# One number in a hand-made instruction order: the scan's positions scaled by 0.75 against attention's

## What is computed

```python
def step(s, inp):                    # one chunk of tokens
    kc, vc, lf = inp[0], inp[1], inp[2]
    cum = jnp.cumsum(lf, axis=2)
    last = cum[:, :, -1:, :]
    s_new = jnp.exp(last[:, :, 0, :])[..., None] * s + \
        jnp.einsum('bhsd,bhse->bhde', kc * jnp.exp(last - cum), vc)
    qc = inp[3]
    o_inter = jnp.einsum('bhtd,bhde->bhte', qc * jnp.exp(cum), s)
    decay = jnp.exp(jnp.where(mask, cum[:, :, :, None, :] - cum[:, :, None, :, :], -jnp.inf))
    att = jnp.einsum('bhtd,bhsd,bhtsd->bhts', qc, kc, decay)
    return s_new, o_inter + jnp.einsum('bhts,bhse->bhte', att, vc)

# per layer, for direction forward and back
mix = jnp.concatenate([fx, ax, rx], axis=-1) @ w_out[l]   # Fourier, attention, scan
```

## Time and profile before

| | us |
|---|---|
| median of 3 executions | 3174.1 (3170.85 to 3175.51) |
| the profiled execution, its own time | 3190.28 |
| its span, first to last instruction | 3188.5 |
| PE, weight loads, DVE, ACT, POOL busy | 2676.0, 2005.8, 783.6, 809.0, 829.6 |

### The profile page before, as it was taken

One profiled execution on the slowest core, in us unless ns is written; L12 is line 12 of the kernel. 1 busy time (PEld: TensorE's weight loads), 2 busy tenths in 40 slices (PEclk: granted clock), 3 DMA queues, 4 the chain that ended last, 5 costly groups with the idle time before them and its releaser, 6 DMA issues.

```text
span 3188.5 us, 38162 instructions
## 1 busy us (share of the span) xinstructions
PE 2676.0 (84%) x16726; PEld 2005.8 (63%) x16726; DVE 783.6 (25%) x1326; ACT 809.0 (25%) x1018; POOL 829.6 (26%) x310
## 2 busy tenths in 40 slices
PE   1898887999995987788769999999695767699997
PEld 0686555777773873334558888888583433577785
DVE  0102323244223004453330111111202453311111
ACT  1232223122123223222232112111323332322222
POOL 0241231333330210233212222222130133244442
PEclk9898898999997997756789999999897778899999
DMA  6231023334441110000201111111011000222221
GB/s 138 99 133 47 21 84 141 140 152 177 156 143 52 53 45 2 1 1 1 79 27 67 53 67 67 53 60 60 27 53 46 1 1 15 92 80 93 104 88 47
DMA packets 42524, 220.55 MB, mean 69 GB/s; under 512 B 4025, under 2 KB 12873, under 8 KB 18933
## 3 DMA queue, kind: packets, MB, share of 16 engines
q1 hardware_dynamic: 35192, 200.52, 17.3%
q10 hardware_dynamic: 7164, 17.57, 2.3%
HBM read 212.05 MB, written 6.03 MB: 68 GB/s over the span
## 4 chain that ended last, share of the span: by engine, by line
PE 70%; DVE 9%; ACT 5%; issue 2%; DMA 1%; POOL 1%; ACTq 0%; DVEq 0%; POOLq 0%
PE PS L590 52%; PE PS L507 2%; PE PS L593 2%; PE PS L935 2%; PE PS L959 2%; PE PS L922 2%; DVE small L1017 1%; PE PS L941 1%; DVE tmp L533 1%; DVE a_lo L525 1%; DVE a_lo L1572 1%; PE PS L1519 1%; PE PS L625 1%; PE PS L1630 1%; DVE hid_lo L766 1%
## 5 line engine op out<-in xcount | busy, mean ns | idle before, releaser
L1758 POOL TENSOR_TENSOR w_lo<-raw,w_hi 128x2048 fp32r<-128x2048 f32 (+1 forms) x146 | 648.5, 4442 | 1653.9 <-ACT w_hi L661 1653.9
L590 PE MATMUL PS<-a_hi,w_hi 128*128 128x512 f32 (+1 forms) x2104 | 678.9, 367 | 162.5 <-DVEq L342 99.7
L590 PE MATMUL PS<-a_lo,w_hi 128*128 128x512 f32 (+1 forms) x2104 | 677.2, 366 | 0.0
L590 PE MATMUL PS<-a_hi,w_lo 128*128 128x512 f32 (+1 forms) x2104 | 674.6, 365 | 0.0
L590 PEld LDWEIGHTS PS<-a_hi,w_hi 128*128 128x128 f32 x2104 | 359.8, 191 | 243.0 <-issue 170.6
L661 ACT ACTIVATE w_hi<-raw 128x2048 fp32r<-128x2048 f32 (+1 forms) x146 | 270.3, 1851 | 523.9 <-PE PS L590 339.9
L590 PEld LDWEIGHTS PS<-a_hi,w_lo 128*128 128x128 f32 x2104 | 360.7, 191 | 66.7
L590 PEld LDWEIGHTS PS<-a_lo,w_hi 128*128 128x128 f32 x2104 | 359.9, 191 | 62.9
L590 PE MATMUL PS<-hid_hi,w_hi 128*128 128x512 f32 (+1 forms) x784 | 269.3, 380 | 36.2 <-DVE hid_lo L766 32.8
L590 PE MATMUL PS<-hid_lo,w_hi 128*128 128x512 f32 (+1 forms) x784 | 266.7, 377 | 0.0
L590 PE MATMUL PS<-hid_hi,w_lo 128*128 128x512 f32 (+1 forms) x784 | 266.2, 376 | 0.0
(11 more groups left out here) (193 smaller groups left out, 2834.5 us busy)
## 6 DMA issues: line engine op xcount, KB each, us to landing
raw<-in_w_ada SPq DMA_DIRECT2D x48, 1024.0 KB, 7.0
raw<-in_w_ff SPq DMA_DIRECT2D x32, 1024.0 KB, 4.8
raw<-in_w_in SPq DMA_DIRECT2D x27, 1024.0 KB, 4.8
raw<-in_w_gate SPq DMA_DIRECT2D x22, 1024.0 KB, 4.7
raw<-in_w_up SPq DMA_DIRECT2D x22, 1024.0 KB, 4.7
raw<-in_w_down SPq DMA_DIRECT2D x16, 1024.0 KB, 4.7
raw<-in_w_out SPq DMA_DIRECT2D x12, 1024.0 KB, 5.0
raw<-in_w_down SPq DMA_DIRECT2D x8, 768.0 KB, 4.2
```

Of the source, the lines that this page charges most:

```text
L590: mm = p.matmul(ps[:, dst], wv[:, k, idx * P:(idx + 1) * P], av[:, k, dst], start=first, stop=last)
L1758: pool.tensor_tensor(w_lo[:, m % 2, 0:kt, 0:ncol], src, w_hi[:, m % 2, 0:kt, 0:ncol].bitcast(F32), ALU.subtract).then_inc(s_lo.sem, 1)
```

## The change

The scan's position is multiplied by 0.75 before it is compared, the other generator's by 1. The diff is whole; the three engines that call `branch` all follow it.

```diff
         def branch(scan, other):
 
 
-            left = [[0.0, 0, scan], [0.0, 1, other]]
+            left = [[0.0, 0, 0.75, scan], [0.0, 1, 1.0, other]]
             while left:
                 head = min(left, key=lambda x: (x[0], x[1]))
                 try:
-                    head[0] = next(head[2])
+                    head[0] = head[2] * next(head[3])
                 except StopIteration:
                     left.remove(head)
```

## The result

The changed kernel is slower. Its median is 3190.8 us (3176.7 to 3204.4, 20 executions) against 3176.0 us (3167.4 to 3190.8, 20 executions) for the kernel before on the same chip; the ratio is 1.0043, with a 95% interval of 1.0029 to 1.0057. That is some 14 us more where I forecast 17 less, and outside the range. Slower had been given a chance of 0.20; the largest part of the loss lies in the first stretch, where the slower rival did not look.

A forecast was written before the change was run, and what follows sets the result against it. The stretches were held bounded by PE, often at 1.2 GHz; -6.2 - 9.9 + 8 + 0 - 9.2 = -17 us took the median from 3174.1 to 3157 us, range 3124 to 3186.

The forecast's parts named there:

- the slower rival: Third stretch's attention: packed scan stops PE more, clock falls from 0.76 to 0.64; +20 us, 3194 us; chance 0.20.
- (1): Ends of all three stretches: the scan's read-out on DVE moves beside attention; minus 6.2 us.
- (2): Ends of second and third stretch: the first w_out panel's transfer starts earlier, leaving the end; minus 9.9 us.
- (3): Second and third stretch, PE: four more scan score/transpose pairs without an attention step between; plus 8 us, ends 0 and 30.
- (4): Second half-scan: four ticks move from attention into rope and Fourier; taken as 0, minus 8 or plus 8 at the ends.
- (5): Second stretch's tail, freed of scan work: two of three slow head pairs run at the high clock; minus 9.2 us.
- the sign named beforehand: Second stretch, profile after: a granted clock over 0.8 in the last 50 us.
- The rule of the Trainium skill: TensorE idling between bursts is throttled and begins each at half rate; closer scan steps would slow the first three quarters.

The follow-up runs named there:

- lead: Against the kernel before: 0.75 in the third stretch alone, attention's position on DVE alone lowered by 0.012 there; 3200.1 us, ratio 1.0076.

## Why the prediction was wrong, step by step

Split by stretch, the forecast was -1.4, -12.1 and -3.8 us; the table says +12.2, -4.6 and +6.7. So 13.6 of the miss of 31.6 us lie in the first stretch, 7.5 in the second and 10.5 in the third.

**The first stretch had no term.** This is the step that failed by most. The sum counts -1.4 us for it (the read-out) and nothing else; scan pieces were costed at where they stand next to each other, in the second and third stretch, and never at what they cover. The scan's work on PE was held to be "the same wherever it stands". It isn't: of three pieces at boundaries, two (outputs and means) stood in a wait that exists without them. In the profile of before the sign was a wait that stood in the list for two boundaries (3.7 us in 2) where the code has five. Measured +12.2 us for the stretch. When only these two pieces move, on PE alone, its one profile has +9.8 (166.0 against 156.2 in the mean, 157.9 at most) and the whole kernel is 0.28% slower: that cost is shown by experiment. What the order of ACT and DVE adds is not settled.

**(1) and (2)** came as given. Between attention's last product and the split of w_out lay 2.3, 7.4 and 8.4 us before, 0.9, 0.6 and 0.9 after: -15.7 for the -16.1 of the sum. With the transfer put back 9.7 us return.

**(3)** sought the price in the wrong row, and too low a price. The wait before line 1491 rose from 0 to 0.5 and from 2.0 to 2.6 us, +1.1 in place of +8 (another 0.8 has no releaser in the profile). But closer steps do cost, two releasers further on: the maxima (line 1017) that stand on DVE behind scan work, +7.6 and +6.6, and the states (line 1320), +2.1 and +4.4. Together with the 1.1 that is 21.8 us of waits, inside the upper end of 30. Against them stand shorter waits for ACT elsewhere in attention. That it is the maxima and states which make the third stretch slower is read from the waits; the runs that moved DVE's order did not turn it into a gain.

**(4)** was put at 0 within 8 either way. In rope and Fourier the waits rose by 8.2 us in the second stretch (18.7 to 23.5 at line 1685, and 3.4 new at line 1630) and by 10.4 in the third; in attention line 922 waits 2.9 and 5.8 less for ACT's roundings. Net some +10 where the two were held to cancel; line 935's shorter waits (0.5 and 3.9) take back 4.4 of it. With the third stretch's front alone packed, the kernel was 0.26% slower. By the term's own formula eleven ticks, not ten, started before 0.24, so three moved and not four.

**(5)** was wrong in its place. The three pairs of 256 columns that end the stretch stayed at the low level, though no scan work lies between them:

```profile
1440.00:1503.00 63.00, 55.22 (x545) 24.74 (x545) 23.54 (x57) 19.09 (x32) 29.40 (x23) 0.86 0.09 33
1503.00:1541.00 38.00, 34.49 (x106) 14.85 (x107) 7.99 (x22) 8.94 (x23) 8.71 (x15) 0.51 0.07 31
```

PE was busy 91% of the second window and the level was 0.51. So the sign named beforehand, over 0.8 in the last 50 us, failed: it was 0.62. The place where the level falls has a stop of PE that the prediction did not look for, and it comes from POOL, whose order is unchanged. POOL is still adding running sums of the wide pairs when the first narrow ones begin, and PE waits for their diagonal matrix:

```profile
1494.04 9.19 POOL L1066 TENSOR_TENSOR acc<-acc,pt 128x512 f32<-128x512 f32 x6
1503.18 0.61 POOL L1052 TENSOR_TENSOR bdiag<-ident,small 128x256 fp32r<-128x256 f32 x1
1503.85 0.58 PE L941 MATMUL PS<-bdiag,ones_r 128*128 128x256 f32 x1 [2.89 <-POOL bdiag L1052]
```

The same product takes 0.38 us at 1500.58 and 0.58 here. All five profiles with 0.75 in the second stretch and no lead have this stop of 2.9 us and the fall behind it, the one with the late transfer too, so the early transfer that runs beside it isn't its cause. With the factors 1, 0.92, 0.92 the level falls at much the same place without it: from 1.00 before 1480 us to 0.50 behind 1485, and PE's longest idle time from 1474 to 1485 is 0.65 us. So a stop of that length isn't needed either, and what holds the level down is open. Yet the second stretch's clock did rise, ahead of the tail: its busy time is 258.9 us in the mean of four profiles with 0.75 (261.9 at most), against 272.0 of twelve with 1 (262.9 at least), a gain of 13 that is more than the 9.2 foreseen. That the term's size was nearly met is luck, since its reason failed. Why the level is higher there no run settles.

**The slower rival** had the right sign. Attention's part of the third stretch fell from 0.76 to 0.71, just under its threshold of 0.72, but with 0.75 in the third stretch alone it is 0.73, and orders that were not changed show 0.69 to 0.76 in that same part. So the fall can't be laid on the change: the means of busy time in the stretch are 206.0 us with 0.75 and 202.6 with 1. That the packed scan stops PE more often did come true (waits for maxima and states); that the clock falls by it isn't shown.

The rule of the Trainium skill named in the prediction ("TensorE: Matmul & The Clock Gate", section "HAM oscillation — how this bites in real kernels") pointed the right way in the first stretch. With PE's two pieces moved and nothing else, two stops of 1.84 us came in, and behind each the level was down for a few us. Clock from 393 to 399 and from 414 to 420 us:

```profile
393.00:396.00 3.00, 3.00 (x14) 2.26 (x14) 0.06 (x1) 0.47 (x2) 0.00 (x0) 0.78 0.00 0
396.00:399.00 3.00, 3.00 (x13) 1.61 (x12) 0.57 (x2) 0.75 (x2) 0.00 (x0) 0.65 0.00 0
...
414.00:417.00 3.00, 3.00 (x12) 2.26 (x13) 1.45 (x3) 1.50 (x3) 0.00 (x0) 0.69 0.00 0
417.00:420.00 3.00, 3.00 (x16) 1.95 (x15) 0.04 (x1) 1.70 (x4) 0.18 (x1) 0.74 0.00 0
```

In the kernel before it was 1.00 from 396.2 us to the stretch's end. An estimate from these four windows: some 6.8 us at the low level, 3.4 us of time, nearly as much as the 3.7 us of the stops themselves. The stretch's busy time read 131.1 us at a clock of 0.80, against 125.6 in the mean of nine profiles with the old order (126.9 at 0.83 in the one shown). The tail of the second stretch agrees with the rule where its level falls, behind a stop of 2.89 us; it doesn't where the level stays at 0.50 for 35 us more with PE's stops at 0.52 us and less.

## What to carry to other kernels

Before moving work out of an interleaved order, ask of each piece not only what it waits for but what wait it fills; look for the repeated wait that is missing in some of its places, since something may stand in it. Keep such pieces there and move only what the end needs: a factor of 0.92 in the last two stretches took read-out and transfer off the end and gained 0.44%, where 0.75 everywhere lost 0.43%. Look also at the engine whose order does not change (here POOL): it may come later for the new order than for the old (PE's stop for it was 1.8 us before and 2.9 after). And an order merged by comparing two numbers reacts in jumps: 0.98 was 10 us slower in its stretch than 1, 0.82 was not, so try several values and read the order that each gives.

## What the runs showed of the hardware

The same instructions in the same order, in the third stretch, took 292.4 to 304.1 us in eight profiles, with a granted clock of 0.74 to 0.68 and PE's idle time nearly unchanged (93.7 to 96.8 us). The kernel before shows it in the windows above, and the kernel with 0.75 in the first stretch alone, whose third is untouched, here:

```profile
2410.50:2711.60 301.10, 207.38 (x1966) 91.82 (x1966) 133.78 (x283) 95.51 (x143) 63.99 (x48) 0.69 0.05 18
```

So one profile can't price a change of 10 us in such a stretch; repeats of the unchanged stretch in other experiments can. And less idle time did not mean that much less time. In the three profiles with 0.92 in the third stretch and no lead, PE idles for 76.5 us in the mean instead of 94.9, but the stretch takes 295.0 us instead of 297.5, since its busy time rises from 202.6 to 218.5 at a clock of 0.66 to 0.67. All three clocks lie under the 0.68 to 0.74 of the eight with factor 1. Why the level is lower there no run settles.
